# Start of a two-block transformer kernel: input loaded by column halves, fewer multiplies of ones, one head copy ahead of a weight rounding

## What is computed

```python
u = rms_norm(h, g_mix[layer])                       # h is x at first
proj = u @ w_in                                     # 1024 x 2208 in the first layer
q_b = proj[..., o3:o3 + nb]                         # o3 = 672, nb = 512
k_b = proj[..., o3 + nb:o3 + 2 * nb]
```

## Time and profile before

| | us |
|---|---|
| median of 3 runs | 973.28 (973.25 to 973.43) |
| the profiled execution, its own time | 973.19 |
| its span in the trace | 971.4 |
| PE busy | 966.5 (99%) |
| DVE busy | 624.0 (64%) |
| ACT busy | 593.1 (61%) |
| data moved | 169.37 MB, mean 174 GB/s |

### The profile page before, as it was taken

How to read it: one execution, slowest core, us unless ns; L and a number is a source line. 1 busy time by engine, 2 the same in 40 slices (tenths; PEclk the granted TensorE clock), 3 DMA queues, 4 the chain that set the end, 5 groups by cost and what they waited for, 6 DMA issues and landing times.

```text
span 971.4 us, 13111 instructions
## 1 busy us (share of the span) xinstructions
PE 966.5 (99%) x4938; PEld 796.0 (82%) x4938; DVE 624.0 (64%) x769; ACT 593.1 (61%) x920; POOL 15.8 (2%) x28
## 2 busy tenths in 40 slices
PE   9999999999999999999999999999999999999998
PEld 7888788888888888788888888888888888888887
DVE  5777766555556767665555555977685667786654
ACT  7777665454545666564545444877667768857571
POOL 2000000000000000000000000000000000000000
PEclk9999999999999999999999999999999999999999
DMA  9545266756564553447666655555534444346651
GB/s 302 165 141 187 87 216 193 241 173 216 173 201 142 178 173 131 131 163 251 219 210 194 226 185 172 174 173 174 174 129 135 150 136 149 131 150 203 208 175 44
DMA packets 106079, 169.37 MB, mean 174 GB/s; under 512 B 4197, under 2 KB 65591, under 8 KB 106033
## 3 DMA queue, kind: packets, MB, share of 16 engines
q1 hardware_dynamic: 103456, 161.23, 50.5%
q0 software_dynamic: 2240, 7.40, 2.3%
q10 hardware_dynamic: 336, 0.10, 0.0%
HBM read 167.56 MB, written 1.16 MB: 174 GB/s over the span
## 4 chain that ended last, share of the span: by engine, by line
PE 97%; SPq 1%; DMA 1%; ACT 1%; issue 0%; DVE 0%; ACTq 0%; DVEq 0%
PE acc L515 14%; PE acc L517 14%; PE acc L516 13%; PE acc L572 12%; PE pair_ps L517 8%; PE pair_ps L515 8%; PE pair_ps L516 7%; PE acc L952 3%; PE acc L635 3%; PE turn_ps L724 2%; PE acc L753 1%; PE turn_ps L590 1%; PE pair_ps L707 1%; PE pair_ps L703 1%; PE turn_ps L515 1%; PE turn_ps L517 1%
## 5 line engine op out<-in xcount | busy, mean ns | idle before, releaser
L2017 DVE TENSOR_TENSOR w_lo<-w_raw,w_hi 128x2048 fp32r<-128x2048 f32 (+3 forms) x154 | 343.2, 2230 | 125.3 <-ACT w_hi L1270 125.1
L1270 ACT ACTIVATE w_hi<-w_raw 128x2048 fp32r<-128x2048 f32 (+3 forms) x154 | 286.5, 1864 | 86.4 <-PE acc L517 39.5
L515 PE MATMUL acc<-w_hi,uT_hi 128*128 128x512 f32 (+3 forms) x456 | 179.5, 394 | 0.2 <-ACT qkv L1357 0.2
L517 PE MATMUL acc<-w_hi,uT_lo 128*128 128x512 f32 (+3 forms) x456 | 174.1, 382 | 0.0
L516 PE MATMUL acc<-w_lo,uT_hi 128*128 128x512 f32 (+3 forms) x456 | 173.7, 381 | 0.0
L515 PE MATMUL pair_ps<-w_hi,uT_hi 128*128 128x512 f32 x320 | 126.5, 395 | 0.0
L517 PE MATMUL pair_ps<-w_hi,uT_lo 128*128 128x512 f32 x320 | 124.8, 390 | 0.0
L516 PE MATMUL pair_ps<-w_lo,uT_hi 128*128 128x512 f32 x320 | 124.6, 389 | 0.0
L515 PEld LDWEIGHTS acc<-w_hi,uT_hi 128*128 128x128 f32 x456 | 85.7, 188 | 19.5 <-issue 4.4
L517 PEld LDWEIGHTS acc<-w_hi,uT_lo 128*128 128x128 f32 x456 | 85.6, 188 | 16.7
L516 PEld LDWEIGHTS acc<-w_lo,uT_hi 128*128 128x128 f32 x456 | 85.9, 188 | 14.1
(11 more groups left out here) (283 smaller groups left out, 1333.5 us busy)
## 6 DMA issues: line engine op xcount, KB each, us to landing
w_raw<-in_w_in SPq DMA_DIRECT2D x46, 1024.0 KB
w_raw<-in_w_gate SPq DMA_DIRECT2D x44, 512.0 KB
w_raw<-in_w_up SPq DMA_DIRECT2D x44, 512.0 KB
w_raw<-in_w_down SPq DMA_DIRECT2D x22, 1024.0 KB
w_raw<-in_w_out SPq DMA_DIRECT2D x12, 1024.0 KB
w_raw<-in_w_qkv SPq DMA_DIRECT2D x16, 512.0 KB
w_raw<-in_w_branch SPq DMA_DIRECT2D x6, 1024.0 KB
w_raw<-in_w_qkv SPq DMA_DIRECT2D x4, 1024.0 KB
```

Of the source, the lines that this page charges most:

```text
L515: mm(o, xh, wh[:, k, :], start=first and k == 0, stop=False)
L517: done = mm(o, xl, wh[:, k, :], start=False, stop=last and k == len(kts) - 1)
L1270: activation(w_hi[:, slot, 0:width], w_raw[:, slot, 0:width], ACT.Copy).then_inc(hi_done, 1)
L2017: v.tensor_tensor(w_lo[:, slot, 0:width], w_raw[:, slot, 0:width], w_hi[:, slot, 0:width].bitcast(f32), ALU.subtract).then_inc(lo_done, 1)
```

## The change

- **Input.** `h` is loaded in two halves by columns (tiles 0 to 3, then 4 to 7, both blocks of tokens), 512 KB each as before. Between the halves stand tiles 0 and 1 of the first unit, behind them tiles 2 and 3. A tile is now one load instead of two. `x_loaded` counts halves.
- **Transposes.** PE transposes the first half (8 instructions) before its first product, and the second half (8 instructions) inside the first unit, ahead of its third tile.
- **Ones.** `keep_busy(8)` becomes 4, `keep_busy(5)` becomes 1.
- **Gains.** The bias table gets a semaphore of its own, `tab_full`; ACT and DVE wait for the gains alone.
- **ACT's order.** `copy(0)` stands ahead of the rounding of the fourth unit, `copy(1)` behind it, and the five `g_col` copies behind that.

```diff
@@ names @@
+        input_tiles_of = [(0, 4), (4, 8)]
...
-        x_loaded = [sem(f"x_loaded{i}") for i in range(TB)]
+        x_loaded = [sem(f"x_loaded{i}") for i in range(2)]
         ident_full = sem("ident_full")
+        tab_full = sem("tab_full")
@@ SyncE @@
-            for blk in range(TB):
-                sp.dma_start(h[:, blk, :], x[0].rearrange("(b p) c -> p b c", p=P)[:, blk, :]).then_inc(x_loaded[blk], 16)
+
+            def input_tiles(i):
+                c = slice(P * input_tiles_of[i][0], P * input_tiles_of[i][1])
+                sp.dma_start(h[:, :, c], x[0].rearrange("(b p) c -> p b c", p=P)[:, :, c]).then_inc(x_loaded[i], 16)
...
-            unit_in_parts(0, [(k, 1, (row_full + raw_full)[k]) for k in range(4)])
+            def tile_of_unit(k, full):
+
+                src = w_in0[k * P:(k + 1) * P, 672:1696].rearrange("p (i c) -> p i c", i=2)[:, :, 0:256]
+                sp.dma_start(view(4, 512)[:, k, :].rearrange("p (i c) -> p i c", i=2), src).then_inc(full, 32)
+
+            input_tiles(0)
+            tile_of_unit(0, row_full[0])
+            tile_of_unit(1, row_full[1])
+            input_tiles(1)
+            tile_of_unit(2, row_full[2])
+            tile_of_unit(3, raw_full[0])
+            n.next_unit()
             unit_in_parts(4, [(0, 2, second_full), (2, 2, raw_full[1])])
@@ TensorE @@
-                    if between and k0:
+                    if between and k0 == 2:
                         between()
...
             def turn_input():
 
                 pe.wait_ge(eps_set, 2)
-                keep_busy(8)
+                keep_busy(4)
                 pe.wait_ge(ident_full, 16)
-                for blk in range(TB):
-                    pe.wait_ge(x_loaded[blk], 16)
-                    for bank, kt0, m in input_banks:
-                        for k in range(m):
+                turn_tiles(0, input_banks[0:3])
+                n.fresh = {kt0: n.bank + i + 1 for i, (_, kt0, _) in enumerate(input_banks)}
+                n.bank = n.bank + len(input_banks)
+                keep_busy(1)
+
+            def turn_tiles(i, banks):
+
+                pe.wait_ge(x_loaded[i], 16)
+                for bank, kt0, m in banks:
+                    for k in range(m):
+                        for blk in range(TB):
                             done = transpose(bank[:, S * k + P * blk:S * k + P * blk + P],
                                              h[:, blk, P * (kt0 + k):P * (kt0 + k) + P], ident[:, :])
-                        if blk == 1:
-                            done.then_inc(turned, 1)
-                n.fresh = {kt0: n.bank + i + 1 for i, (_, kt0, _) in enumerate(input_banks)}
-                n.bank = n.bank + len(input_banks)
-                keep_busy(5)
+                    done.then_inc(turned, 1)
...
-                    pe.wait_ge(gains_full, 32)
+                    pe.wait_ge(tab_full, 16)
...
-                unit_in_parts(0, [(k, 1, first_lo, k + 1) for k in range(3)] + [(3, 1, lo_done, 1)])
+                unit_in_parts(0, [(k, 1, first_lo, k + 1) for k in range(3)] + [(3, 1, lo_done, 1)],
+                              lambda: turn_tiles(1, input_banks[3:5]))
                 unit_in_parts(4, [(0, 2, first_lo, 4), (2, 2, lo_done, 2)], distances)
@@ ScalarE @@
-            act.dma_start(tabT[:, :], rel_col).then_inc(gains_full, 16)
+            act.dma_start(tabT[:, :], rel_col).then_inc(tab_full, 16)
...
                 scaled_by(MIX0)
-                slot_step(1536)
                 copy = heads_copy(0)
                 copy(0)
+                slot_step(1536)
                 copy(1)
+                for group, row in enumerate((0, 2, 2, 2, 4)):
+                    done = activation(g_col[:, 2 * group:2 * group + 2], gain_T[:, QK_COL + row:QK_COL + row + 2], ACT.Copy)
+                link(done)
                 slot_step()
...
-            act.wait_ge(gains_full, 32)
+            act.wait_ge(gains_full, 16)
...
+            for full in x_loaded:
+                act.wait_ge(full, 16)
             for blk in range(TB):
-                act.wait_ge(x_loaded[blk], 16)
                 row_squares(MIX0, h, D, blk)
...
-            for group, row in enumerate((0, 2, 2, 2, 4)):
-                done = activation(g_col[:, 2 * group:2 * group + 2], gain_T[:, QK_COL + row:QK_COL + row + 2], ACT.Copy)
-            link(done)
@@ VectorE @@
-            dve.wait_ge(gains_full, 32)
+            dve.wait_ge(gains_full, 16)
```

## The result

| | median, us | runs, us |
|---|---|---|
| before | 973.41 | 11, 972.94 to 973.51 |
| changed | 975.61 | 11, 975.08 to 976.39 |

The ratio is 1.0024, 95% interval 1.0016 to 1.0032: slower by 2.2 us. Forecast were 976.5 us and a range of 973.9 to 977.3. The changed kernel's runs also lie further apart, 1.3 us against 0.6.

A forecast was written before the change was run, and what follows sets the result against it. PE, busy 99% of the span and without a wait after 20.70 us, was taken as the bound, so the start decides. Terms a to e sum to +1.3, with f +3.2: 976.4 us profiled, 976.5 against the median; range 973.9 to 977.3.

The forecast's parts named there:

- f: Before and during the first products: fewer ones let PE's clock rise only at 11.7, products at half pace; +1.9 us.
- a: At the start: ACT begins when the gains land (6.10), so the first product comes at 7.91; -0.45 us.
- b: Between second and third tile: eight transposes, formerly in waiting time, now stand in PE's stream; +0.85 us.
- c: After the moved transposes: PE waits shortly for the split of tiles 4 and 5; +0.1 us.
- d: After the second unit: PE's wait for ACT's head copy goes, as the copy precedes the rounding; -0.3 us.
- e: At PE's turns: later rounding and split delay DVE's table addition that frees `acc[2]`, a new PE wait; +1.1 us.
- The first rival: At the first products: the clock is up in time, f is 0 to 0.5, time 974.6 to 975.1; 38 in 100.
- The rest: One load for two, tabT's own semaphore, POOL's loads about 1.4 us later: costs nothing.

The follow-up runs named there:

- e11: Changed kernel with DVE's table addition ahead of its fourth-unit split, and 8 multiplies of ones ahead of the transposes, 1 behind: 973.29 us.
- e1: Kernel before with ACT's new order alone (head copy ahead of the fourth unit's rounding, gain copies last): 974.16 us, ratio 1.0009.
- e2: Changed kernel with DVE's addition to the table moved ahead of its split of the fourth unit: 974.56 us.
- e3: Changed kernel with 8 and 5 multiplies of ones again instead of 4 and 1: 974.64 us, ratio 1.0012.
- e4: Changed kernel with both the table's addition first and 8 and 5 multiplies of ones: 973.32 us, ratio 1.0000.
- e6: Changed kernel with 8 multiplies of ones again ahead of the transposes and still 1 behind: 974.64 us.
- e10: e4 with the eight transposes of the second half, inside the first unit, made twice: 974.19 us, 0.87 above e4.
- e5: Kernel before with 4 and 1 multiplies of ones instead of 8 and 5, nothing else: 973.53 us against 973.30.

## Why the prediction was right, and where it was off

The forecast was slower, for the right causes, with one of them too large: 976.5 against 975.61. Luck had a part in it. That the time would lie clear of no change hung on f, which no row settled: without f the forecast's own sum gives 974.6, below the 975.2 from which it counts a change. f was taken at its upper end, came out at half of that, and the time lies 0.4 us above the bound.

- **What bounds the kernel.** Right: PE has no wait behind the turns in either kernel, and the 2.46 us at the turns arrive whole (2.45 in the time).
- **a, first product earlier.** Forecast -0.45, measured -0.67. The step that failed is the gains' landing as the bound: they landed 4.0 us after their issue, at 5.2, and the first half of the tokens at 5.0. What bound it was this half: PE transposed from 5.16 at the slow pace, and ACT followed the first two transposes at 5.92. The issues, for the earlier trace rows:

```profile
w_raw<-in_w_in SPq DMA_DIRECT2D x8, 256.0 KB, 6.8
...
h<-in_x SPq DMA_DIRECT2D x2, 512.0 KB, 5.3
...
gain_T<-in_gains_col ACTq DMA_DIRECT2D x1, 29.5 KB, 4.0
```

The loads of 256 KB took 6.8 us in the median instead of 4.5 for the loads of 128 KB; why, no run separates. The third tile of the first unit was the late one, and ACT waited for it to 9.36. In the changed kernel that cost nothing, because PE came to that tile only at 12.42; in e11, with the pace up, it cost the 0.2 us named there.
- **b, transposes in the stream.** Forecast +0.85, measured 0.79 in the profile and 0.87 by doubling. They ran at 0.10 each, the quick pace. By the Trainium skill's sentence (TensorE: Matmul & The Clock Gate, Part 4: PE-mode transpose) that the full clock doesn't engage for transposes they would have cost 1.7; this case's traces disagree, with 0.10 each.
- **c, tiles 4 and 5.** Forecast +0.1, measured 0.23, of which some 0.1 is the longer first distance behind the transposes; a further 0.16 in the next stretch I had not counted: 0.11 of it is the longer first distance behind the wait (15.37 to 15.71, 0.34 instead of 0.23).
- **d, head copy.** Forecast -0.3, measured -0.31.
- **e, table.** Forecast +1.1, and the same wait came by e1 alone. Measured 1.05 by e2's median, 1.27 by its distances and 1.3 by the two quieter pairs: the place and the cause were right, the size up to 0.2 short.
- **f, fewer ones.** Forecast +1.9, measured 1.07 in the profile, 0.97 by e3, and 1.24 from e2 to e4. The mechanism was right and the size was not. The step that failed is "if it rises only after 3.8 us of unbroken work", which put the rise at 11.7. It came at 10.0 to 10.2, although PE's work was broken by 0.2 us of standing still. That pause was expected to be 1.0 us: the input came 0.44 later than I had assumed (5.16 instead of 4.72), so the transposes and ones ended later, and the first product came 0.2 earlier. How long PE had worked before the rise isn't the same in all kernels either: from 1.15 to 4.95, 3.8 us, in the kernel before; from 5.16 to about 10.0, 4.8 us, here. e6 shows that a pause of 0.83 us does no harm once the pace is up; what such a pause does before the rise, no run shows. The first rival, that the clock is up by the first product, didn't happen in the changed kernel.
- **The rest.** POOL's loads came 2.5 us later (8.89 instead of 6.40) and not 1.4. Nothing came of it: the one-hot table is used at 18.35.

With f at 1.0 and a at -0.67 the forecast's own sum gives 973.19 + 2.1 = 975.3 against 975.64.

What stays open is why the moment of the rise differs between executions of one kernel. In the kernel before it was 4.95; in e1, the same up to there, the transposes at 5.00 are still 0.21 apart and those from 5.64 on 0.11. With the new loads and eight ones ahead it came within the ones in e11, between the transposes of 5.6 and 6.4 in e3, and only behind them, past 6.8, in e4. The spreads of the times fit that (e2 2.3 us and the changed kernel 1.3, with four ones; e4 0.45 and e10 0.7, with eight), but e5, with four ones and the old loads, spreads over 0.8 only, and no experiment set the moment by itself.

## What to carry to other kernels

When an instruction is moved ahead on an engine that runs its list in order, ask what was queued behind it and who waits for that: moving one copy ahead of a rounding saved PE 0.3 us and made it wait more than 1 us for an addition on another engine, two steps on. Work that fills waiting time is free only there; the eight transposes stood in such time ahead of the first product, and cost 0.8 us behind it, more than the 0.67 us that the earlier start gave. Idle multiplies that hold the pace up may be cut only with an eye on the distances of the first real products, not on the busy time, and on enough executions to see their spread.

## What the runs showed of the hardware that was not expected

- Four multiplies of ones (1.7 us of work at 1.2 GHz) followed by a pause of 1.9 us were worth no more than none: 975.61 and 975.72. Eight (3.6 us), followed by 0.2 us of pause, brought the time down by 1.0.
- The pace rises at different moments in different executions of the same instructions: at 4.95 us in the kernel before and at about 5.6 in e1; before 4.8 in e11 and past 6.8 in e4. The granted clock reads 1.00 in all of them; only the distances show the rise.
- Transposes of 128x128 in float32 stand 0.10 us apart at the quick pace (e10, behind 10.59) and 0.21 at the slow one (behind 5.61 in the changed kernel).
- The gains, 29.5 KB on ACT's queue, landed 0.9 us earlier (4.0 instead of 4.9 us) when only SP's loads were cut and ordered differently.
